# Dilated attention heads in a two-block fp32 kernel: bands of 64 tokens and classes modulo four in place of full score tiles

## The reference

```python
DIL_PATTERNS = ((128, 1), (512, 4), (2048, 16))
# query t attends to t + j*dilation for j in [-r, r], r = window // (2*dilation)
s = q.k / 8 - slope * dilation * |rel|      # only where |rel| <= r
m, e, l = max(s), exp(s - m), sum(e)
o, lse = e @ v / l, m + log(l)              # one of each per pattern
w = softmax(lses over the three patterns);  out = sum(w * outs)
```

## Time and profile before

| | us |
|---|---|
| median of three runs (2962.22 to 2965.35) | 2964.47 |
| profiled execution: span | 2964.6 |
| PE busy in the span | 2829.0 |
| DVE, ACT, POOL busy | 1777.5, 1073.4, 905.5 |

### The profile page before, as it was taken

The page is one execution under the profiler, slowest core; times in us unless marked ns, Lnnn a source line. Parts: engine busy times, 40 slices in busy tenths (PEclk is TensorE's granted clock), DMA queues, the critical chain, the costliest instruction groups (busy, mean ns, idle before and its releaser), DMA issues. The chain is left out here.

```text
span 2964.6 us, 39168 instructions
## 1 busy us (share of the span) xinstructions
PE 2829.0 (95%) x15342; PEld 2108.9 (71%) x15342; DVE 1777.5 (60%) x2635; ACT 1073.4 (36%) x1763; POOL 905.5 (31%) x531
## 2 busy tenths in 40 slices
PE   6999999999998999999999999979999999997999
PEld 5879797977877777777767877646666655554677
DVE  5787878785012344444453126667667777886686
...
GB/s 163 59 82 72 86 65 92 65 72 198 132 117 79 37 51 44 51 51 51 51 15 163 79 107 194 127 49 15 42 42 59 19 56 55 59 19 78 191 154 113
DMA packets 114310, 241.24 MB, mean 81 GB/s; under 512 B 9168, under 2 KB 52944, under 8 KB 114128
## 3 DMA queue, kind: packets, MB, share of 16 engines
...
## 5 line engine op out<-in xcount | busy, mean ns | idle before, releaser
L79 PE MATMUL psum<-u_h,w_hi 128*128 128x512 f32 (+2 forms) x2624 | 1008.4, 384 | 22.0 <-DVE u_h L2674 6.0
L80 PE MATMUL psum<-u_h,w_hi 128*128 128x512 f32 (+2 forms) x2624 | 968.3, 369 | 0.0
L81 PE MATMUL psum<-u_h,w_lo 128*128 128x512 f32 (+2 forms) x2624 | 966.5, 368 | 0.0
L135 POOL TENSOR_SCALAR w_hi<-w_raw 128x1024 fp32r<-128x1024 f32 x212 | 247.1, 1165 | 1515.9 <-ACTq L1324 520.0
L79 PEld LDWEIGHTS psum<-u_h,w_hi 128*128 128x128 f32 x2624 | 497.5, 190 | 165.6 <-issue 84.9
L137 POOL TENSOR_TENSOR w_lo<-w_raw,w_hi 128x1024 fp32r<-128x1024 f32 x212 | 544.6, 2569 | 17.7
L81 PEld LDWEIGHTS psum<-u_h,w_lo 128*128 128x128 f32 x2624 | 497.6, 190 | 71.4
L80 PEld LDWEIGHTS psum<-u_h,w_hi 128*128 128x128 f32 x2624 | 498.0, 190 | 67.0 <-issue 6.3
L2550 DVE TENSOR_TENSOR a_exp<-psum,a_strips 128x1024 f32<-128x1024 f32 x128 | 156.4, 1222 | 133.9 <-PE psum L2229 132.6
L2393 ACT ACTIVATE a_exp<-a_exp 128x1024 f32<-128x1024 f32 x128 | 135.6, 1059 | 244.1 <-DVE a_exp L2550 244.1
L1349 ACT ACTIVATE f_exp<-psum 128x1024 f32<-128x1024 f32 (+4 forms) x112 | 82.1, 734 | 192.9 <-PE psum L1207 94.0
...
## 6 DMA issues: line engine op xcount, KB each, us to landing
...
```

Of the source, the lines that this page charges most:

```text
L79: nc.tensor.matmul(out, w_hi[:, k], a_hi, start=(k == 0 and first), stop=False)
L80: nc.tensor.matmul(out, w_hi[:, k], a_lo, start=False, stop=False)
L81: return nc.tensor.matmul(out, w_lo[:, k], a_hi, start=False, stop=(k == kk - 1 and final))
L135: self.nc.gpsimd.tensor_scalar(self.hi[:, r], self.raw[:, r], 1.0, 1.0, ALU.mult, ALU.mult).then_inc(self.hi_done, 1)
```

## The change

A dilated pass is worked off in 8 units instead of 16. Units 0 to 3 hold two "band" blocks each, units 4 to 7 two "perm" blocks. A band block is 128 tokens in their own order as keys, against 64 rows of each of the four classes modulo four as queries, the ones around it (256 columns). A perm block is 128 keys of one class against that class's 256 queries. For this Q and K are stored by class (POOL reads with a step of four elements), with a second copy in token order (`tok`): first Q for the band maxima, later K for the band scores (`key_tokens`). V is transposed a second time by class (`P`). The products of `keys` take 8 pieces of two blocks, with 256 columns each, all in steps 8 to 13 of loop q-1; their maxima are transposed twice (`EB`, `EP`), 8 transposes each, and DVE merges them (`merge_rows`) at step 15, before the pass's first scores. Scores of unit u stand at step 2u of the pass's own loop, its value product at the end of step 2u+2, that of the last at step 15. The outputs of both halves are complete only at the end; the first half's denominator and inverse move from step 8 to 13 and later. In the last loop the eighth result therefore comes after the loop, and the output projection does seven of eight k for both tiles and then the last k for both. Differential passes have Q in two whole buffers instead of three halves, and four gate buffers instead of three; strips shrink to one DMA per pass.

```diff
...
+    base = lambda p: U * min(p, DIFF) + U // 2 * max(p - DIFF, 0)
+    UNITS = base(PASSES)
+    pass_of = lambda X: (X // U, X % U) if X < base(DIFF) else (DIFF + (X - base(DIFF)) // 8, X % 8)
+    AQ = T // 4
+    first_of = lambda kb: min(max(32 * kb - 16, 0), AQ - 64)
+    band_at = lambda kb: first_of(kb) - 32 * kb + 32
+    LISTS = [("band", 0, 1), ("band", 2, 3), ("perm", 0, 1), ("perm", 2, 3), ("band", 4, 5), ("band", 6, 7), ("perm", 4, 5), ("perm", 6, 7)]
...
-        if x == 8 and p >= 0 and not diff(p):
+        if x == 13 and p >= 0 and not diff(p):
             out.append(("D", p, 0))
+        if x in (0, 2) and p >= 0 and not diff(p):
+            out.append(("P", p, x // 2))
         if q < PASSES:
             if x in sums_of(q):
                 out.append(("S", q, sums_of(q)[x]))
-            if x == (12 if q else 3):
-                out.append(("T", q, 0))
+            if x == (3 if q == 0 else 12 if diff(p) else 13):
+                out.insert(0, ("T", q, 0))
             if x == 14:
-                out.append(("E", q, 0))
+                out.append(("E", q, 0) if diff(q) else ("EB", q, 0))
+            if x == 15 and not diff(q):
+                out.append(("EP", q, 0))
...
+    def scored(p, x):
+
+        if p >= DIFF:
+            return base(p) + x // 2 if x % 2 == 0 else None
+        X = U * p + x + 1
+        return X if 0 <= X < base(DIFF) else None
+
+    def valued(p, x):
+
+        if 0 <= p < DIFF:
+            return U * p + x
+        if p >= DIFF and (x == U - 1 or x % 2 == 0 and x > 0):
+            return base(p) + (7 if x == U - 1 else x // 2 - 1)
+        return None
 
     def pieces(p, x):
 
-        if x < 5 and p >= 0:
+        if x < 5 and p >= 0 and diff(p):
             return [(p, 11 + x)]
         if p < 0:
             return [(0, a) for a in {8: [0], 9: [1], 10: [2, 3], 11: [4, 5], 12: [6, 7], 13: [8], 14: [9], 15: [10]}.get(x, [])]
-        return [(p + 1, a) for a in pass_pieces.get(x, [])] if p + 1 < PASSES else []
+        if p + 1 >= PASSES:
+            return []
+        at = pass_pieces if diff(p + 1) else {8: [0], 9: [1], 10: [2, 3], 11: [4, 5], 12: [6], 13: [7]}
+        return [(p + 1, a) for a in at.get(x, [])]
...
+        def blocks(u):
+
+            return [("band", 2 * u), ("band", 2 * u + 1)] if u < 4 else [("perm", 2 * u - 8), ("perm", 2 * u - 7)]
+
+        def chosen(t, own, kind, b):
+
+            return own[:, P * b:P * b + P] if kind == "band" else t[:, AQ * (b // 2) + P * (b % 2):AQ * (b // 2) + P * (b % 2) + P]
+
+        def reached(t, kind, b):
+
+            return rows_of(t, b) if kind == "band" else t[:, AQ * (b // 2):AQ * (b // 2) + AQ]
+
+        def bias_of(q, kind, b):
+
+            t = strips[:, q % 2, 0:1536].rearrange("p (j c) -> p j c", j=2)
+            if kind == "band":
+                return t[:, :, 0:384].rearrange("p j (c a) -> p j c a", c=4)[:, :, :, band_at(b):band_at(b) + 64]
+            return t[:, :, 512 - P * (b % 2):512 - P * (b % 2) + AQ]
...
-                    n = 2 * q + g - GQ0
-                    hi, lo = q_hi[:, n % 3], q_lo[:, n % 3]
-                    least(pool, st_ok, 16 * (q - 1) + (8 if g == GQ1 else 0))
+                    hi, lo = q_hi[:, q % 2], q_lo[:, q % 2]
+                at, new = slice(512 * (g % 2), 512 * (g % 2) + 512), un[:, c % 2]
+                hi, lo = (t[:, at] if diff(q) else classes(t)[:, :, P * (g % 2):P * (g % 2) + P] for t in (hi, lo))
+                if not diff(q):
+                    new = turned(new)
+                least(pool, st_ok, base(q - 1) if q else 0)
                 pool.wait_ge(un_ok, c + 1)
-                nc.gpsimd.tensor_copy(hi, un[:, c % 2]).then_inc(hi_ok, 1)
+                nc.gpsimd.tensor_copy(hi, new).then_inc(hi_ok, 1)
+                if g in (GQ0, GQ1) and q >= DIFF:
+                    if q > DIFF:
+                        pool.wait_ge(st_ok, base(q - 1) + 4)
+                    nc.gpsimd.tensor_copy(tok[:, 0, at], un[:, c % 2]).then_inc(tok_ok, 1)
                 pool.wait_ge(hi_ok, c + 1)
-                nc.gpsimd.tensor_tensor(lo, un[:, c % 2], hi.bitcast(F32), ALU.subtract).then_inc(lo_ok, 1)
+                nc.gpsimd.tensor_tensor(lo, new, hi.bitcast(F32), ALU.subtract).then_inc(lo_ok, 1)
+
+            def key_tokens(q, i):
+
+                pool.wait_ge(lo_ok, 4 * q + 4)
+                pool.wait_ge(mx_full, base(q) + 6)
+                source = (k_hi, k_lo)[i][:, q % 2].bitcast(F32)
+                nc.gpsimd.tensor_copy(turned(tok[:, i]), classes(source)).then_inc(tok_ok, 1)
...
+                if kind == "P":
+                    for c in range(4):
+                        last = nc.tensor.transpose(bank[:, P * c:P * c + P], turned(vT[:, g])[:, c], K.ident[:, :])
...
+                if kind in ("EB", "EP"):
+                    for b in range(8):
+                        n = 2 * b + (16 if kind == "EP" else 0)
+                        to = ps[:, MX + P * b:MX + P * b + P]
+                        last = nc.tensor.transpose(to, mn[:, n:n + P], K.ident[:, :])
...
+                if not diff(q):
+                    if a == 0 and q > DIFF:
+                        pe.wait_ge(sfree, number[("S", q, GQ1)] + 1)
+                    if a in (0, 4):
+                        pe.wait_ge(tok_ok, 4 * (q - DIFF) + 1 + a // 4)
+                    for s, b in enumerate(LISTS[a][1:]):
+                        for j in range(2):
+                            r, at = slice(64 * j, 64 * j + 64), MX + 512 * j + AQ * s
+                            mine, seen = list_tile(q_hi[r, q % 2], tok[r, 0], a, b), list_reach(k_hi[r, q % 2], a, b)
+                            last = nc.tensor.matmul(ps[:, at:at + AQ], mine, seen, start=True, stop=True)
+                    last.then_inc(mx_full, 1)
+                    return
...
+                if not diff(p):
+                    if u == 0:
+                        pe.wait_ge(tok_ok, 4 * (p - DIFF) + 4)
+                    for s, (kind, b) in enumerate(blocks(u)):
+                        out = lambda j: ps[:, ST + 512 * j + AQ * s:ST + 512 * j + AQ * s + AQ]
+                        rows = lambda j: slice(64 * j, 64 * j + 64)
+                        for t, (ka, qa, i) in enumerate([(k_hi, q_hi, 0), (k_hi, q_lo, 0), (k_lo, q_hi, 1)]):
+                            for j in range(2):
+                                nc.tensor.matmul(out(j), chosen(ka[rows(j), p % 2], tok[rows(j), i], kind, b), reached(qa[rows(j), p % 2], kind, b),
+                                                 start=(t == 0), stop=False)
+                        for j in range(2):
+                            every = eq[rows(j)].rearrange("p h c -> p (h c)")
+                            last = nc.tensor.matmul(out(j), ek[rows(j), :], reached(every, kind, b), start=False, stop=True)
+                    last.then_inc(st_ok, 1)
+                    return
...
+            def spread(X, p, u):
+
+                if u == 0:
+                    pe.wait_ge(sfree, number[("EP", p, 0)] + 1)
+                    pe.wait_ge(o_ok, 2 * p)
+                if u == 2:
+                    pe.wait_ge(sfree, number[("T", p, 1)] + 1)
+                if u == 4:
+                    pe.wait_ge(sfree, number[("P", p, 1)] + 1)
+                pe.wait_ge(exp_ok, X + 1)
+                for s, (kind, b) in enumerate(blocks(u)):
+                    for h in range(2) if kind == "band" else [b // 4]:
+                        for j in range(2):
+                            out = ps[64 * j:64 * j + 64, OB + 512 * h:OB + 512 * h + 512].rearrange("p (c a) -> p c a", c=2)
+                            w = pt[:, X % 3, j, AQ * s:AQ * s + AQ]
+                            if kind == "band":
+                                last = nc.tensor.matmul(out[:, :, first_of(b):first_of(b) + 64], V[:, b, j], classes(w)[:, 2 * h:2 * h + 2],
+                                                        start=(b == 0), stop=False, skip_group_check=True)
+                            else:
+                                last = nc.tensor.matmul(out[:, b // 2 % 2], V_p[:, b // 2, b % 2, j], w,
+                                                        start=False, stop=(b % 4 == 3), skip_group_check=True)
...
-            for u in range(2):
-                W.wait(pe, 0, 0, 36 + u)
-                for k in range(KT):
-                    if u == 0:
-                        pe.wait_ge(mix_lo, k + 1)
-                    last = gemm_k(nc, ps[:, 512 * u:512 * u + 512], W.hi[:, u], W.lo[:, u], u_hi[:, k, 0:512], u_lo[:, k, 0:512], k)
-                if u == 0:
-                    last.then_inc(gfull, 1)
+            pe.wait_ge(add_ok, UNITS)
+            for ks in (range(LAST), [LAST]):
+                for u in range(2):
+                    W.wait(pe, 0, 0, 36 + u)
+                    for k in ks:
+                        if u == 0:
+                            pe.wait_ge(mix_lo, k + 1)
```

(60 more changed lines are left out.)

287 lines of the change are left out of this document (159 added, 128 removed).

## The result

| | before | after |
|---|---|---|
| median | 2963.64 us (2962.22 to 2965.35, 4 runs) | 2912.77 us (2910.43 to 2914.46, 4 runs) |
| profiled span | 2964.6 us | 2911.0 us |
| ratio | | 0.983, 95% interval 0.9815 to 0.9843 |
| PE busy | 95% | 95% |

What follows compares the result with a forecast made beforehand. PE was taken to bound loops 3 to 6, and loop 7 only after its opening. Loops 4 to 6 -42.3, loop 3 +0.6, loop 7 -23.5 and the end +3 make -62 from 2964.6: 2902 us, range 2874 to 2932.

Steps and rivals of the forecast that it cites:

- PE's work in loops 4 to 6: Per loop, scores gain 8.3 us, keys 2.6 and values 7.3, transposes lose 2.2: 16.0 us less PE work.
- What becomes late: New PE waits in loops 4 to 6, 1.9 us a loop, leaving a gain of 14.1 a loop.
- step (2): Keys in steps 10 and 11: DVE's reductions take longer than the projections beside them; 1.5 us more PE waits a loop.
- step (3): `merge_rows`, last in DVE's step 15, precedes the next scores; taken as just covered, 0 to 3 us.
- step (1): Denominator wait, 1.2 us before: no keys stand ahead of it any more, so 0.4 us more a loop.
- makes any wait on ACT unlikely: Value products stand two steps behind their exponentials, so PE should hardly wait for ACT; no time was added.
- So loops 3 to 6 are PE's: PE sets these loops before the change; a shorter DVE is worth nothing there by itself.
- the first rival: Keys, maxima, transposes, merge and scores set the loops, not PE: 5 us more in four loops, 2922 us; chance 0.19.
- the credit's 3 us: At the phase's end, credit for the next phase's first weights comes later, so POOL's split ends later: 3 us longer.
- Other costs of the ending I put at nothing: After the last value product, costs besides the late weights credit were taken as covered by the same projections: 0 us.
- The rule on steps above 8 bytes: POOL's stepped reads of Q and K would cost some 5 us more a loop; the sum was left unchanged.
- The fourth rival: POOL's stepped access makes POOL the bound; all gain is lost at a cost multiple of 5.4, 2992 us at 6; chance 0.04.

Runs made afterwards that it cites:

- the other order: Against the changed kernel with both ending repairs, key pieces in loop 3 alone stand in steps 8, 9, 9, 10, 11, 11, 12, 13; 2899.11 us.
- the credit's edit: Against the changed kernel, the output projection does all eight k of its first weight tile, then all eight of the second; 2909.19 us.
- the one with other keys: Against the changed kernel, key pieces in all loops stand in steps 8, 9, 9, 10, 11, 11, 12, 13; 2910.71 us.

## Why the prediction was right, and where it wasn't

Right as a whole: 2912.8 lies in the range, and most of the gain is where it was put. But 62 us were forecast and 50.9 came; 14.1 are missing by stages, and untouched phases made 11 of them. By its own steps:

**PE's work in loops 4 to 6**: 17.4 us less a loop at the full clock, predicted 16.0. Within it errors of both signs partly cancel. Added up from start to start without the waits, in the trace of before and the second of after, scores gained 7.5 us a loop (8.3 predicted), keys 2.5 (2.6), values 8.4 (7.3), transposes lost 1.5 (2.2), and 0.5 came elsewhere. Scores (1.14 a unit, not 1.06) and keys (0.43 a piece, not 0.34) have a change of array shape on the way out that I counted only on the way in; the old keys were dearer than I had them too, 6.0 us a loop and not 5.3. Values are cheaper: band and perm units both cost 1.02 us, 1.11 with the way in, where I had 1.38 and 1.20. For the band unit I had taken 0.31 for four records of 128 columns from the row of 144; they take a quarter of 1.02. Eight transposes take 0.79 instead of 1.1.

**"What becomes late", the term that was mis-sized**: 1.9 us predicted, 4.3 measured, 7.2 us too little in three loops. The greater gain in PE work gives 4.2 of them back, and the lower clock in loop 6 takes 1.45; that leaves the 4.4 us that loops 4 to 6 are short. Its three parts hold. Waits at the keys grew from 1.0 to 2.5 us a loop (4.5 + 1.8 + 1.2 over three), by just the 1.5 of step (2); the merge of step (3) is covered; the denominator's wait of step (1) grew by 0.2 for 0.4. What failed is the sentence behind them, that the lagging value product "makes any wait on ACT unlikely". It looked at the exponentials only. The waits that ACT ends grew from 0.6 to 3.3 us a loop: squares 1.8 (before 0.6), a bank that ACT must empty ahead of a denominator 0.7, ahead of `P` 0.5, and one for `a_classes` 0.3. The last three, 1.5 us together, come with the new order and not with less work: a denominator's product now stands directly behind V's transposes and `P` directly behind a denominator, and both need the small bank that ACT is still copying. For the squares, that the removed work had been their cover is argued and not shown by itself; what is shown is that 1 us of other work taken from in front of them, in the odd steps, lengthens them from 5.5 to 8.5 us.

**"So loops 3 to 6 are PE's"**: true of the kernel before, and used one step too long. After the change PE is busy for 78 of 85 us, but no longer sets the loop alone: 1.9 us of PE work taken from a loop shortens it by 0.65, 7.9 of DVE by 1.2, and a chain through ACT and POOL that is opened at both places by 1.7. This isn't the first rival, "the chain decides", either. Its price was 5 us in each of four loops (2922); loops 3 to 6 stand 6.6 us in all above the forecast (4.4 and 2.2), and 3.1 of these are stretches at the lower clock (1.45 in loop 6, 1.6 in loop 3). Of its long waits for DVE and the merge, the maxima have 1.5 us a loop (2.1 with those that have no releaser), and the merge none. The loops lie between the two, nearer the forecast, and the chain that was found is another one, from the squares on ACT through DVE's scaling and POOL's split to the keys.

**Loop 3**: +2.8 and not +0.6. The 2.1 us are one wait for maxima, which step (2) had as about 1, and behind it stands a stretch at the lower clock; the other order gives 94.4, 0.2 below the loop before the change.

**Loop 7**: -23.9 against -23.5, with the first `embed` 19.2 us into the loop (18 predicted) and 41.3 us behind it (43). That the sum is so near is luck: two misses of 1.2 and 1.7 us nearly cancel, and the clock alone moves this loop by 1 us.

**The end**: the credit's 3 us were 3.2. "Other costs of the ending I put at nothing, since the same projections cover them" is the second step that failed, by some 8 us: 2.2 of wait for the numerator's buffer (2.98 where the kernel before has 0.74), 2.7 of lower clock behind it, and 2.8 in the tail (186.6 against 183.8), most of it lower clock behind the wait for the credit; the credit's edit alone won back 2.4. I had checked that the last result comes in time for the projection; I hadn't asked what its first step, the copy, waits for. It waits for DVE to finish the other half, since both halves now end together and share one buffer. The 2.7 is the difference between this stage in the changed kernel (26.9) and in the one with other keys (24.2), whose ending has the same code and the same wait of 2.98 us: the granted clock was 0.50 from 2699.7 to 2706.5 in the one and 1.00 at this place in the other. Why it fell in one and not the other stays open.

**The rule on steps above 8 bytes** (the Trainium skill, GPSIMD Engine Reference, section 7: about half as much again) was weighed and left the sum as it was. The rows have 34% on the subtraction, 80% on the casts that read so. It isn't hidden: the access is worth 0.9 us in loop 4 by itself and, with ACT's order repaired, 5 us in three loops. The fourth rival, POOL as the bound, stays far off at 32 us of 85.

**DVE near 52** was wrong too: 62.9 us in loop 5. The sums of the exponentials, which I had halved, take 20.2 us in that loop, as in the kernel before (L2625 and L2628 there; L2816, L2817 and L2820 now, 0.66 us for an add of 256 columns, 0.82 for a copy). Part of that comes from POOL beside them, as the last section shows.

What isn't settled: why loop 6 has a stretch at the lower clock in one profile of the changed kernel and not in the other.
